# Where eight attention units divide by their softmax sums: on the exponentials, or on the outputs

## The chip, the cores and the metric

One Trainium2 chip, one core. The metric is device time in microseconds (us) of one execution, and the kernel before takes 1225.23 us (median of three runs, 1224.18 to 1225.33). Engine names are those of the profile: PE is the matrix engine (PEld its weight loads), DVE the vector engine, ACT the scalar engine, POOL the GpSimd engine, SP the queue that issues most DMAs.

## The reference, cut to what matters

The kernel computes a two-layer encoder trunk over 1024 positions of width 1024. Layer 0 mixes with differential attention (A, 4 heads of width 128) and sliding-window attention (B, 8 heads). Layer 1 mixes with chunked attention over a band of nine chunks of 64 positions (C, 16 heads of width 64). The change touches C alone:

```python
def chunked_relpos_attention(q, k, v, rel_table):      # per chunk c of 64 queries
    s = jnp.einsum('bqhd,bkhd->bhqk', qb, kb).astype(jnp.float32) * scale + bias
    valid = (c * CHUNK - pad + j) >= 0
    s = jnp.where(valid, s, NEG)
    p = jax.nn.softmax(s, axis=-1)
    return jnp.einsum('bhqk,bkhd->bqhd', p.astype(vb.dtype), vb)
# around it, layer 1:
    proj = jnp.einsum('bsd,de->bse', h, w_in_c[i])
    qc, kc, vc, gc = jnp.split(proj, 4, axis=-1)
    y = jnp.einsum('bse,ed->bsd', yc * jax.nn.silu(gc), w_out_c[i])
    x = x + rms_norm(y, post_norm_g[l])
```

The softmax is exp(s - max) divided by its row sum, and the division may stand before or after the product with v.

## The kernel before, in words

**Units.** The work is cut into 20 units: A0 to A3, B0 to B7 and C0 to C7. A C unit is one pair of heads over all 1024 positions. It has 16 items, one for each head h and each tile t of 128 queries, in the order (h0,t0) (h0,t1) (h1,t0) (h1,t1) (h0,t2) and so on (`order`, L85). An item of a C unit sees one to five tiles of 128 keys, most of them five.

**Steps.** All engines walk through one list of steps, each engine in its own fixed order, and wait for one another by semaphores. A C unit starts every 20 steps. Items run in its steps 0 to 15, and steps 16 to 19 hold the projections of keys and queries for the next unit. The pipeline of an item that is scored in step s, for a unit that is not "deferred":

- PE scores it in step s (`score`, L1309, matmuls at L1339) from q and k into PSUM.
- DVE adds the bias and finds the row minimum of the negated scores in its step s+1 (`lowest`, L1757, instruction L1771, into e_sb). ACT takes the exponential in its step s+1 (`exp`, L1443, L1447) and sums the rows into `total`.
- DVE in its step s+2 takes the reciprocal of the sum (L1783) and multiplies the exponentials by it in place (`normalise`, L1775, L1787).
- PE transposes the tiles in step s+3 (`turn`, L1273, L1306) into PSUM `turned`. ACT copies them rounded (L1480) and DVE keeps the remainder (L1836), both in step s+4.
- For each head and pair of query tiles PE multiplies by v one step after the second transpose (`times_v`, L1231, L1259). ACT and DVE then add the two halves of the result into `o_sb` (L1495, L1844).

For a "deferred" unit (`deferred`, L55) the multiplication at L1787 does not happen. The transposes come one step earlier, in step s+2, and the product with v with them. For each pair of query tiles, that is four times in a C unit, once both heads are there:

- DVE takes four reciprocals in one instruction (`denominators`, L1798, L1811).
- ACT spreads them over 256 columns (`widen`, L1514, L1520, into `rec_wide`).
- PE transposes these in two instructions (`turn_rec`, L1263, L1270) into the half of `pv_ps` that the product with v is not about to use.
- DVE multiplies `o_sb` by them (`times_rec`, L1813, L1819).

B0 to B7, C0 and C7 are deferred before. C1 to C6 are not.

**The order within a step on PE** is written out at L1366 to L1389: its share of the projections (`project`, L1126), one product with the output weights of the unit before (`spare_use`, L1140, matmuls L1137), the transposes of one item, the scores of one item, `turn_rec`, the product with v, and in the last step of a unit the transposes of the next unit's v (L1294).

**Between two C units.** In step 20 DVE keeps the remainder of v (L1831). In step 21 it multiplies the finished `o_sb` by the gate (`gated`, L1869, L1886), then ACT rounds it (`hi_of_gated`, L1497, L1512) and DVE takes the remainder (`gated_lo`, L1889, L1897). The first product with the output weights of the finished unit stands in step 4 of the next unit, and it waits for two things: that remainder, and the unit's output weights. Those weights are loaded by SP (L860) into a buffer that comes free with the last output product of the step before (step 19), and POOL splits them into a rounded part and a remainder (`split`, L967, one instruction at L971 and four at L978):

```python
            if x.what == "out":
                for u, w in zip(x.units, x.blocks):
                    if new(w_ready, PRO_SPLITS + w.n + 1):
                        pe.wait_ge(w_ready, PRO_SPLITS + w.n + 1)
                    if new(s_ylo, gate_of(u, x.row) + 1):
                        pe.wait_ge(s_ylo, gate_of(u, x.row) + 1)
```

On ACT the gated rounding of step 21 stands behind the first exponential of the unit and ahead of the second. On DVE the gated product stands behind item 0's row minimum and ahead of item 1's.

Of the kernel before, what the change touches and what calls it, by code (L numbers as in the profile page):

```python
# [33 lines left out]
            C=dict(q=0, k=1024, v=2048, g=3072))  # L34
# [5 lines left out]
class Unit:  # L40
# [12 lines left out]

    @property
    def deferred(self):  # L55
        return self.kind == "B" or self.kind == "C" and self.i in (0, 7)

    def slope(self, h):
        if self.kind == "A":
# [37 lines left out]
B = [Unit("B", i, 80 + 8 * i) for i in range(8)]  # L97
BRIDGE = 11
C = [Unit("C", i, 80 + 64 + BRIDGE + 20 * i) for i in range(8)]
# [1965 lines left out]
```

## Time and profile before

| | before |
|---|---|
| median of 3 runs | 1225.23 us |
| the profiled execution, its own time | 1223.95 us |
| its span, first to last instruction | 1222.2 us |
| PE busy | 1182.2 us (97%) |
| DVE busy | 804.6 us (66%) |
| ACT busy | 588.9 us (48%) |
| POOL busy | 432.8 us (35%) |
| granted PE clock, mean | 0.995 |

The span is what the instructions fill, and the execution's own time is 1.75 us more. The four engines run side by side, so their busy times are not to be added. Matmuls overlap in the records: a 128x512 matmul is shown with some 0.39 us, but the next one starts 0.23 us after it, so what a matmul costs PE is read from the distance between two starts. The C units lie from about 592 us to the end, and C1 to C6 start at about 669, 749, 827, 906, 984 and 1063 us, C7 at 1141.5 us.

### The profile page before, as it was taken

Reading aid. Unit: us, or ns where it says so; the run is one execution under the profiler, and the core shown is the slowest. Engines: PE = TensorE matmul, PEld = TensorE weight load, DVE = VectorE, ACT = ScalarE, POOL = GpSimd, SP = SyncE. Lnnn points to the kernel's source line nnn. Section 1 sums busy time; section 2 is a strip of 40 time slices with the busy share of each in tenths; the row PEclk is TensorE's granted clock in tenths of the full one; section 3 lists DMA queues with packets and bytes.
Section 4 is the critical chain, followed back from the end, with each engine's and each line's share of the span. In section 5 each row is a group of like instructions: output and inputs, shape, how many; then the busy total and the mean of one; then the engine's idle time right before and its main releaser. Section 6 shows DMA issues by size and latency. Waiting matters only on the chain.

```text
span 1222.2 us, 17651 instructions
## 1 busy us (share of the span) xinstructions
PE 1182.2 (97%) x6492; PEld 1006.7 (82%) x6492; DVE 804.6 (66%) x1708; ACT 588.9 (48%) x1296; POOL 432.8 (35%) x557
## 2 busy tenths in 40 slices
PE   7999999999999999898999999999999999999995
PEld 6988888888888887787788888888888888888873
DVE  5464765757767768867553866848658577585585
ACT  5554444434444556655454444534434444454463
POOL 5333214133172465556752114124141241412312
PEclk9999999999999999999999999999999999999998
DMA  6261101011021153245221102011020110201026
GB/s 197 67 192 44 60 18 52 18 53 35 18 87 53 51 156 104 69 127 155 61 77 58 34 21 71 18 56 53 18 74 19 56 53 19 73 18 57 18 47 109
DMA packets 93559, 78.42 MB, mean 64 GB/s; under 512 B 3073, under 2 KB 83969, under 8 KB 93474
## 3 DMA queue, kind: packets, MB, share of 16 engines
q1 hardware_dynamic: 92466, 73.63, 19.9%
q0 software_dynamic: 1008, 3.67, 1.9%
q8 instruction: 52, 0.85, 0.3%
q14 instruction: 33, 0.27, 0.1%
HBM read 68.85 MB, written 13.68 MB: 68 GB/s over the span
## 4 chain that ended last, share of the span: by engine, by line
PE 48%; DVE 2%; issue 1%; ACT 1%; POOL 1%; POOLq 0%; DVEq 0%; ACTq 0%
PE dense L1126 25%; PE dense L1137 7%; PE pv_ps L1259 6%; PE scores L1339 4%; PE turned L1306 4%; PE turned L1294 0%; DVE pT_lo L1836 0%; ACT k_hh L1440 0%; DVE e_sb L1771 0%; POOL w_lo L978 0%; POOL rowstat L1004 0%; DVE fin L2032 0%; PE scores L1137 0%; ACT junk L1622 0%; POOL rowstat L1001 0%
## 5 line engine op out<-in xcount | busy, mean ns | idle before, releaser
L1126 PE MATMUL dense<-hT_hi,w_hi 128*128 128x512 f32 x880 | 350.5, 398 | 0.0
L1126 PE MATMUL dense<-hT_lo,w_hi 128*128 128x512 f32 x880 | 344.6, 392 | 0.0
L1126 PE MATMUL dense<-hT_hi,w_lo 128*128 128x512 f32 x880 | 344.2, 391 | 0.0
L971 POOL TENSOR_SCALAR w_hi<-w_f 128x1024 fp32r<-128x1024 f32 x86 | 93.0, 1081 | 642.4 <-PE dense L1126 585.2
L978 POOL TENSOR_TENSOR w_lo<-w_f,w_hi 128x256 fp32r<-128x256 f32 x344 | 264.8, 801 | 7.2
L1447 ACT ACTIVATE e_sb<-e_sb,low 128x256 f32<-128x256 f32 (+7 forms) x256 | 170.3, 665 | 172.5 <-DVE low L1771 170.1
L1480 ACT ACTIVATE pT_hi<-turned 128x640 fp32r<-128x640 f32 (+3 forms) x224 | 117.2, 523 | 165.3 <-PE pv_ps L1259 94.5
L1126 PEld LDWEIGHTS dense<-hT_hi,w_lo 128*128 128x128 f32 x880 | 165.4, 188 | 36.6
L1126 PEld LDWEIGHTS dense<-hT_hi,w_hi 128*128 128x128 f32 x880 | 166.0, 189 | 26.1 <-issue 0.3
L1126 PEld LDWEIGHTS dense<-hT_lo,w_hi 128*128 128x128 f32 x880 | 166.2, 189 | 25.1
L1836 DVE TENSOR_TENSOR pT_lo<-turned,pT_hi 128x640 fp32r<-128x640 f32 (+3 forms) x224 | 133.5, 596 | 39.1 <-ACT pT_hi L1480 38.9
L1771 DVE CUSTOM_DVE_ANT_0 e_sb<-scores,bias 128x640 f32<-128x640 f32 (+3 forms) x192 | 131.4, 685 | 41.8 <-PE scores L1339 39.9
L1259 PE MATMUL pv_ps<-pT_hi,v_st 128*128 128x256 f32 x536 | 128.5, 288 | 1.7 <-DVE pT_lo L1836 1.7
L1339 PE MATMUL scores<-k_hh,q_st 128*128 128x384 f32 (+3 forms) x352 | 126.0, 358 | 0.7 <-DVE low L1771 0.6
L1306 PE MATMUL turned<-ident,e_sb 128*128 128x128 f32 x744 | 118.1, 273 | 1.7 <-DVE pT_lo L1836 1.3
L1306 PEld LDWEIGHTS turned<-ident,e_sb 128*128 128x128 f32 x744 | 92.7, 140 | 29.8 <-DVE pT_lo L1836 5.5
L1259 PE MATMUL pv_ps<-pT_lo,v_st 128*128 128x256 f32 x456 | 117.1, 283 | 0.0
L1339 PE MATMUL scores<-k_l,q_st 128*128 128x384 f32 (+3 forms) x352 | 107.7, 315 | 0.0
L1259 PEld LDWEIGHTS pv_ps<-pT_hi,v_st 128*128 128x128 f32 x536 | 97.6, 191 | 3.9 <-DVE pT_lo L1836 2.5
L1697 DVE TENSOR_TENSOR k_l<-dense,k_hh 64x512 fp32r<-64x512 f32 x48 | 33.0, 688 | 94.2 <-ACT k_hh L1440 93.7
L1691 DVE SCALAR_TENSOR_TENSOR q_st<-dense,q_st 64x512 fp32r<-64x512 f32 x60 | 41.4, 689 | 79.6 <-ACT q_st L1434 79.2
L1735 DVE TENSOR_TENSOR y<-dense,y 128x512 f32<-128x512 f32 x108 | 74.2, 687 | 23.9 <-PE dense L1137 23.0
(215 smaller groups left out, 1796.7 us busy)
## 6 DMA issues: line engine op xcount, KB each, us to landing
w_f<-in_w_in_c SPq DMA_DIRECT2D x37, 512.0 KB, 4.1
w_f<-in_w_in_ab SPq DMA_DIRECT2D x34, 512.0 KB, 3.9
rel_tiles_dram<-rel_rows_dram SPq DMA_DIRECT2D x1, 5120.0 KB, 23.8
bias<-rel_tiles_dram SPq DMA_DIRECT2D x8, 640.0 KB, 5.5
y<-in_x SPq DMA_DIRECT2D x8, 512.0 KB, 8.0
hT_lo_f<-in_x SPq DMA_DIRECT2D x8, 512.0 KB, 7.2
out_x<-y SPq DMA_DIRECT2D x8, 512.0 KB, 3.9
w_f<-in_w_out_c SPq DMA_DIRECT2D x8, 512.0 KB, 3.7
```

Source lines behind the costliest of these rows:

```text
L971: ts(hi, src, 1.0, 1.0, ALU.mult, ALU.mult).then_inc(w_hi_done, 1)
L978: last = tt(lo[:, h, cols], src[:, h, cols], hi[:, h, cols], ALU.subtract)
L1126: last = mm(dense[:, x.n % 2, :], lhs[:, d * P:(d + 1) * P], rhs[:, d, x.f * HALF:(x.f + 1) * HALF], start=i == 0, stop=i == 23)
L1137: last = mm(bank, lhs[:, c:c + P], rhs, start=not begun and m == n == 0, stop=m == len(parts) - 1 and n == 2)
L1259: last = mm(pv_ps[:, p.n % 2, :], v_st[:, which, kt, :], p_part[:, kt - p.t + 6 - pT_set(p), :], start=i == 0 and m == 0, stop=i == p.coun ...
L1306: last = nc.tensor.transpose(turned[:, at0:at0 + P], e_sb[:, e0:e0 + P], ident[:])
L1339: last = mm(scores[:, at0:at0 + w], q_st[:, it.h, c:c + P], k_part[:, kh, key:key + w], start=i == 0, stop=i == 1)
L1447: copy(e, e, ACT.Exp, scale=-1.0, bias=stat_col(low, it.j), accum_out=stat_col(total, it.j)).then_inc(s_exp, 1)
L1480: copy(pT_parts(pv)[0][:, r, q], turned_tile(x), ACT.Copy).then_inc(s_thi, 1)
L1735: last = tt(into, dense[:, 2, :], into, ALU.add)
L1771: nc.vector.tensor_tensor_reduce(out=e_of(it), in0=scores[:, it.off:it.off + it.n * P], in1=bias_of(it), scale=-u.slope(it.h), scalar=star ...
L1836: tt(lo[:, r, q], turned_tile(x), hi[:, r, q], ALU.subtract).then_inc(s_tlo, 1)
```

## The change

The property that decides which units are deferred now names every C unit. Everything else follows from it when the step lists are built (L234, L244, L255).

```diff
     @property
     def deferred(self):
-        return self.kind == "B" or self.kind == "C" and self.i in (0, 7)
+        return self.kind == "B" or self.kind == "C"
```

So in C1 to C6 the instructions at L1783 and L1787 go, those at L1811, L1520, L1270 and L1819 come, and transposes and products with v stand one step earlier.

## Rows read from the trace of the kernel before

**Rows 1.** Stretch of C5: its length, busy PE, PEld, DVE, ACT, POOL, then clock.

```profile
984.00:1062.00 78.00, 78.00 (x426) 66.68 (x425) 53.02 (x117) 35.66 (x74) 21.59 (x27) 1.00 0.14 43
```

**Rows 2.** Who PE waited for, from 590 to 1135 us (the one row).

```profile
PE dense L1137 <- DVE y L1733: 0.4, 1, 0.4
```

**Rows 3.** DVE groups of C5, 984 to 1062 us: count, busy us, mean ns.

```profile
L1787 DVE TENSOR_SCALAR e_sb<-e_sb,rec 128x640 f32<-128x640 f32 (+4 forms) x16 | 8.8, 552 | 0.6
L1783 DVE RECIPROCAL rec<-total 128x1 f32<-128x1 f32 x16 | 2.4, 153 | 0.0
```

**Rows 4.** Groups of the whole trace, shapes kept apart.

```profile
L1270 PE MATMUL pv_ps<-ident,rec_wide 128*128 128x128 f32 x48 | 9.2, 272 | 0.0
L1819 DVE TENSOR_TENSOR o_sb<-o_sb,pv_ps 128x256 f32<-128x256 f32 x24 | 10.1, 421 | 2.8 <-DVE o_sb L1844 0.5
L1811 DVE RECIPROCAL rec<-total 128x4 f32<-128x4 f32 x8 | 1.3, 168 | 0.0
L1520 ACT ACTIVATE rec_wide<-rec 128x256 f32<-128x256 f32 x24 | 9.9, 412 | 4.2 <-DVE rec L1811 3.7
```

**Rows 5.** Timeline of PE in C0: start us, length us, instruction.

```profile
627.73 0.38 PE L1270 MATMUL pv_ps<-ident,rec_wide 128*128 128x128 f32 x2
627.86 0.36 PE L1259 MATMUL pv_ps<-pT_hi,v_st 128*128 128x256 f32 x1
```

**Rows 6.** Timeline of PE from C3's last step into C4.

```profile
903.60 0.28 PE L1259 MATMUL pv_ps<-pT_hi,v_st 128*128 128x256 f32 x1
...
905.03 1.04 PE L1294 MATMUL turned<-ident,vT 128*128 128x128 f32 x8
...
912.10 0.27 PE L1306 MATMUL turned<-ident,e_sb 128*128 128x128 f32 x1
...
913.58 0.39 PE L1126 MATMUL dense<-hT_hi,w_lo 128*128 128x512 f32 x1
913.89 0.47 PE L1137 MATMUL dense<-w_hi,yT_hi 128*128 128x512 f32 x1
```

**Rows 7.** Timeline of SP and POOL over the same stretch.

```profile
903.79 0.34 SPq L860 DMA_DIRECT2D w_f<-in_w_out_c  x1
...
904.31 2.82 POOL L978 TENSOR_TENSOR w_lo<-w_f,w_hi 128x256 fp32r<-128x256 f32 x4
907.81 1.06 POOL L971 TENSOR_SCALAR w_hi<-w_f 128x1024 fp32r<-128x1024 f32 x1 [0.68 <-DMA w_f<-in_w_out_c]
908.95 4.84 POOL L978 TENSOR_TENSOR w_lo<-w_f,w_hi 128x256 fp32r<-128x256 f32 x4
```

**Rows 8.** Timeline of DVE and ACT over the same stretch.

```profile
905.77 0.69 DVE L1735 TENSOR_TENSOR y<-dense,y 128x512 f32<-128x512 f32 x1
907.16 1.23 DVE L1831 TENSOR_TENSOR v_st<-turned,v_st 128x1024 fp32r<-128x1024 f32 x1 [0.70 <-ACT v_st L1463]
909.08 1.69 DVE L1886 SCALAR_TENSOR_TENSOR o_sb<-o_sb,gate 128x1024 f32<-128x1024 f32 x1
911.90 1.30 DVE L1897 TENSOR_TENSOR yT_lo<-o_sb,yT_hi 128x1024 fp32r<-128x1024 f32 x1 [0.39 <-ACT yT_hi L1512]
...
910.80 1.06 ACT L1512 ACTIVATE yT_hi<-o_sb 128x1024 fp32r<-128x1024 f32 x1 [1.11 <-DVE o_sb L1886]
911.77 0.49 ACT L1447 ACTIVATE e_sb<-e_sb,low 128x256 f32<-128x256 f32 x1
```

**Rows 9.** The same POOL group two boundaries later (C5 to C6).

```profile
1066.01 4.84 POOL L978 TENSOR_TENSOR w_lo<-w_f,w_hi 128x256 fp32r<-128x256 f32 x4
```

**Rows 10.** Timeline of PE, from C0 into C1 and from C6 into C7.

```profile
673.88 0.39 PE L1126 MATMUL dense<-hT_hi,w_lo 128*128 128x512 f32 x1
674.18 0.33 PE L1339 MATMUL scores<-k_hh,q_st 128*128 128x128 f32 x1
...
1144.97 0.39 PE L1126 MATMUL dense<-hT_hi,w_hi 128*128 128x512 f32 x1
1145.46 0.44 PE L1339 MATMUL scores<-k_hh,q_st 128*128 128x384 f32 x1
```

## The prediction

> **What bounds the kernel now.** I read the stretches of the C units first. From 984 to 1062 us, about the length of C5, PE is busy for 78.00 of 78.00 us while DVE has 53.02 and ACT 35.66 [rows 1]. PE's granted clock is 1.00 there. The waits of PE say the same from the other side: over all of C0 to C6 they hold one row, 0.4 us [rows 2]. So in C1 to C6, where the change acts, PE is the bound and is fed without a gap. Work that leaves DVE returns at most what PE waits for, which is next to nothing. Whatever is added to PE, or makes it wait, lengthens the kernel by its full amount, because nothing behind it is idle to catch up. Then I read the timeline of PE, SP, POOL, DVE and ACT over one boundary between two units, C3 to C4 [rows 6 to 8], because this is where the order of the work is changed most.
>
> **What goes.** In each of six units DVE loses 16 multiplications (8.8 us) and 16 reciprocals (2.4 us) [rows 3], 11.2 us a unit and 67 us together. All of it lies beside PE's work, so I count nothing for it. A few small waits of PE go with it. The 0.4 us [rows 2] is a wait for DVE's addition into y in C1's step 5. PE also starts some 0.1 to 0.2 us late at the same place of three later units, and the transposes of C1's first item wait for a multiplied tile. I put all of these at -1.2 us, and the bounds are 0 and -1.5.
>
> **What comes, on DVE and ACT.** Four times a unit, 24 times in all, DVE gets a reciprocal of four columns (0.168 us) and a product of 128x256 (0.421 us), and ACT a spreading copy (0.412 us) [rows 4]. That is 14.1 us of DVE against 67 removed, and 9.9 us of ACT, which is idle for more than half of the stretch [rows 1]. I count both at nothing. They are hidden by PE's projections, and if that cover were gone the largest single piece would be the 0.42 us on the way to the next product with v (a rival below).
>
> **What comes, on PE: the turned reciprocals.** The records give 272 ns to each of the two transposes [rows 4], but records on PE overlap. What counts is by how much the next instruction starts later: the pair starts at 627.73 and the product with v behind it at 627.86 [rows 5], so a pair costs 0.13 us. 24 pairs are **3.1 us**, all on the path.
>
> The Trainium skill (TensorE: Matmul & The Clock Gate, Part 4: PE-mode transpose) gives a transpose of 128x128 about 275 ns in a kernel's context. The record's length agrees with it, the distance of the starts does not. By the page's figure as a price the term would be 13.2 us in place of 3.1, by the start distances it is 3.1. That reading is a rival below.
>
> **What moves: the last product with v of a unit.** Transposes and products come one step earlier. In the steady part of a unit each step keeps its content on PE: six projection matmuls, one output product, one item's transposes, one item's scores, and every second step a product with v. The short step between two transposes (the one without a product) had just enough time for row minimum, remainder and transposes, and it now has more, since the multiplication no longer stands ahead of them on DVE. Nothing is counted for these steps.
>
> At the end of a unit it is different. The last product with v stood in step 19, between the last output product and the transposes of the next v: 903.60 to 905.03, 1.43 us [rows 6]. Now it stands in step 18, so PE arrives at everything in the next unit 1.43 us earlier as seen from the end of the step-19 output product. Other engines do not come earlier with it. That output product frees the weight buffer. SP issues the load of the finished unit's output weights at 903.79, POOL starts at 907.81 behind the DMA, and its four remainders last from 908.95 to 913.79 [rows 7]. PE needs these weights for the first output product in step 4, which starts at 913.89, 0.31 us behind the matmul before it where 0.23 is usual [rows 6]: it is already on the edge. The start of this chain hangs on an instruction that the change leaves in place.
>
> POOL's group takes 4.84 us where the same group takes 2.82 with DVE otherwise occupied [rows 7]. In that stretch DVE has two products with two operands in SBUF, L1886 with 1.69 us and L1897 with 1.30 us [rows 8], and each holds one POOL instruction up by about 1 us. Both remain. The gated product starts earlier, in the middle of POOL's first instruction, and I expect both still to meet POOL. The group lasts 4.84 us in another boundary also [rows 9].
>
> So in the changed kernel PE resumes at the same 913.89, with 1.43 us less work done in between and one more pair of transposes (those of item 1, now in step 3, 0.13 us as in [rows 5]). The loss is 1.43 - 0.13 = 1.3 us at most for one boundary.
>
> The other chain to step 3 and 4 gives the lower bound. PE wants to transpose item 1 where it transposed item 0, 912.10 - 1.43 = 910.67 [rows 6]. It needs the exponential of item 1, which ACT runs behind the rounding of the gated output (910.80, then 911.77 [rows 8]), and that waits for the gated product on DVE. The remainder of v (907.16) can start only 0.7 us earlier, since an addition into y of 0.69 us from 905.77 stands ahead of it on DVE [rows 8], and the addition of the last product's halves, about 0.4 us, is gone from between. The gated product then starts near 909.08 - 0.7 - 0.4 = 908.0, ends near 909.4, 1.4 us earlier than before, and item 1's exponential is finished near 911.1. PE loses 0.4 us by this chain alone. The two are in series on PE, so the later one decides: between 0.4 and 1.3 us. I take 1.2, near the upper end, because the buffer, the DMA and POOL's own work do not move. What is late next is the weights' remainder, not the exponential. The boundaries C1 to C2, up to C5 to C6, are five: **6.0 us**.
>
> C0 to C1 and C6 to C7 are different. C0 was deferred before, so nothing of its end moves, but C1's first two items are transposed a step earlier. PE's scores already start at 674.18, 0.30 us behind the matmul before them [rows 10], held by item 0's minimum. The transposes behind them wait for exponentials that end some 0.5 us later, twice, so about +1.0 us. Into C7 the last product of C6 moves away. The scores of item 1 start at 1145.46, 0.49 us behind the matmul before [rows 10], and would wait for the minimum of item 0 a little longer, +0.3 us. C7 needs C6's weights only in its step 8.
>
> **Sum:** 3.1 + 6.0 + 1.3 - 1.2 = 9.2 us. The profiled execution has 1223.95 us, so it would be 1233.1. The median lies 1.28 above that execution, and the forecast for a median is 1234.4 us.
>
> **The rivals.** *Only the transposes.* If POOL's remainders do not meet the two DVE products any more, they end up to 2 us earlier and the boundary costs nothing but the exponential's 0.4 us or less. With the small gains this is 3.1 + 0 to 2.0 + 1.3 - 1.2, 3.2 to 5.2 us if the exponential counts, and down to 2 us if that is off as well, some 1227.2 to 1230.4 us. For it speaks that PE's other waits are so small. Against it, that the DMA and POOL are tied to step 19. Chance 0.15.
>
> *Faster.* The relief of DVE would have to reach PE at one place: the remainder of a transposed item (L1836), on which the next transposes wait. It decides if PE's records hide waits there. Were a tenth of the 67 us taken from DVE on this path, it would be -6.7 + 3.1 = -3.6, 1221.6 us. Against it: 78.00 of 78.00 busy [rows 1] and a single 0.4 us [rows 2]. Chance 0.03.
>
> *A new wait in each pair.* The product with v that follows a `turn_rec` waits for DVE's multiplication by the reciprocals. If its 0.421 us [rows 4] came on top 24 times, the time would be 10.1 us more, 1244.5. In C0 this wait exists and PE has no row for it [rows 2]. Chance 0.05.
>
> *Transposes at their full length.* 48 x 0.272 = 13.1 us in place of 3.1 [rows 4] gives 1244.4. The 0.13 us of [rows 5] speak against it. The page named above would have it so. Chance 0.02.
>
> **The numbers.** The forecast has 0.75. Its own range is 1231 to 1237 us, and down to 1228 takes in most of the first rival. I close the upper end at 1239, which leaves the last two out. A measurement of this kernel can tell about 0.2%, 2.5 us, from no change. Faster is the second rival, 0.03. Within 0.2% is the lower part of the first, 0.05. The rest, 0.92, is slower.
>
> **What would show it.** PE's busy matmuls at L1270 go from 48 to 96. DVE's busy time falls by some 50 us and the span grows all the same. At each of five boundaries PE shows an idle stretch before L1137 or L1306, of together more than 1 us, and in the first C step 4 of a unit the end of L978 lies just ahead of L1137. Within a unit, from step 5 on, PE has no wait. I am wrong if the five boundaries are free of waits (then it is near 1228), or if L1270 or the L1259 behind it shows waits in mid-unit.

## The result and the profile after

The changed kernel takes 1234.34 us (median of four runs, 1233.45 to 1235.39) against 1224.96 us of the kernel before in the same session. The ratio is 1.0079, its 95% interval 1.0063 to 1.0094. It is slower by 9.4 us, and the forecast was 1234.4. The profiled execution has 1233.45 us and a span of 1231.7 us. The sum came out right, but not because each of its terms did. Two of them, the price of a pair and the boundaries, were off in opposite directions. A third, the small waits that go, was larger than I allowed for. The runs below put sizes on them. Of the eight executions of the first run without reciprocals, three took 1475 to 4238 us and are left out of its median below.

First the busy times of the changed kernel, from its page, and the transposed reciprocals from its groups (engine, count, busy us, mean ns):

```profile
PE 1189.1 (97%) x6540; PEld 1013.1 (82%) x6540; DVE 763.0 (62%) x1564; ACT 594.1 (48%) x1320; POOL 430.6 (35%) x557
...
L1270 PE MATMUL pv_ps<-ident,rec_wide 128*128 128x128 f32 x96 | 18.3, 272 | 0.0
```

DVE gave up 41.6 us of its 804.6 and the kernel became longer. (The prediction had some 50, and by the sum of the records it is 52.8. Neighbouring records on DVE overlap, and the busy time counts that once.) PE has 48 matmuls more, all at L1270, where 48 became 96 as against [rows 4].

Who PE waited for from 590 to 1145 us, where [rows 2] has one row of 0.4 us:

```profile
PE dense L1137 <- issue: 2.0, 2, 1.0
PE turned L1306 <- ACT e_sb L1447: 1.6, 5, 0.5
PE dense L1294 <- DVE hT_lo L1747: 0.2, 1, 0.2
```

The two places named in the prediction are there: the transposes of the first items, which wait for ACT's exponential, and the first output product of a unit. "Issue" means that the view found no releaser. The boundary from C3 to C4 shows what it was. PE, then POOL, then DVE and ACT, to be laid beside [rows 6 to 8] (what follows the step-19 output product starts at 909.33 here and at 903.60 there, so everything is to be read 5.73 us later):

```profile
909.33 1.03 PE L1294 MATMUL turned<-ident,vT 128*128 128x128 f32 x8
...
918.14 0.39 PE L1126 MATMUL dense<-hT_hi,w_lo 128*128 128x512 f32 x1
919.55 0.47 PE L1137 MATMUL dense<-w_hi,yT_hi 128*128 128x512 f32 x1 [1.02 <-issue]
```

```profile
909.52 0.34 SPq L860 DMA_DIRECT2D w_f<-in_w_out_c  x1
...
913.57 2.00 POOL L971 TENSOR_SCALAR w_hi<-w_f 128x1024 fp32r<-128x1024 f32 x1 [0.70 <-DMA w_f<-in_w_out_c]
915.66 3.79 POOL L978 TENSOR_TENSOR w_lo<-w_f,w_hi 128x256 fp32r<-128x256 f32 x4
```

```profile
913.45 1.22 DVE L1886 SCALAR_TENSOR_TENSOR o_sb<-o_sb,gate 128x1024 f32<-128x1024 f32 x1
...
915.79 1.68 DVE L1897 TENSOR_TENSOR yT_lo<-o_sb,yT_hi 128x1024 fp32r<-128x1024 f32 x1 [0.78 <-ACT yT_hi L1512]
```

The v transposes now follow the output product directly, at 909.33. Before, a product with v of 1.43 us stood between. POOL's remainders end at 915.66 + 3.79 = 919.45 and PE's output product starts at 919.55, 1.18 us later than the 0.23 us rhythm would have it. The gated remainder on DVE had been done since 917.47. So PE waited for the weights, as forecast.

The boundary from C1 to C2 goes another way:

```profile
756.27 0.40 PE L1126 MATMUL dense<-hT_hi,w_lo 128*128 128x512 f32 x1
756.96 0.33 PE L1306 MATMUL turned<-ident,e_sb 128*128 128x128 f32 x1 [0.29 <-ACT e_sb L1447]
...
758.63 0.40 PE L1126 MATMUL dense<-hT_hi,w_lo 128*128 128x512 f32 x1
759.11 0.47 PE L1137 MATMUL dense<-w_hi,yT_hi 128*128 128x512 f32 x1
```

```profile
753.20 1.05 POOL L971 TENSOR_SCALAR w_hi<-w_f 128x1024 fp32r<-128x1024 f32 x1 [0.35 <-DMA w_f<-in_w_out_c]
754.34 4.67 POOL L978 TENSOR_TENSOR w_lo<-w_f,w_hi 128x256 fp32r<-128x256 f32 x4
...
753.42 1.90 DVE L1886 SCALAR_TENSOR_TENSOR o_sb<-o_sb,gate 128x1024 f32<-128x1024 f32 x1
```

Here POOL's first instruction came 0.22 us ahead of the gated product instead of 0.12 us behind it. It took 1.05 us and not 2.00, but it stretched the gated product to 1.90 us, and everything behind that product (rounding, item 1's exponential) is late. PE waits 0.46 us for the exponential and 0.25 us for the weights. (These sizes are start distances: 756.96 - 756.27 = 0.69 us, where 0.23 is usual. The view's 0.29 is only the part in which no matmul record runs.) The two waits are not independent. POOL's last remainder ends 9.71 us after the start of the v transposes (759.01 - 749.30), against 10.12 us from C3 to C4 (919.45 - 909.33), and PE goes on right behind it both times. So the weights decide the sum of the waits, 0.7 or 1.2 us, and the wait for the exponential lies inside it. By start distances the five boundaries cost 0.71, 0.69, 1.18, 0.73 and 1.19 us, **4.5 us** in all. In C1 the first two items wait 0.68 and 0.35 us for their exponentials. All the small waits that stood in C1 to C6 before are gone: 0.9 us in C1, 0.1 to 0.3 us in each of the others, **1.9 us** in all.

### The profile page after: what moved, and what is told of

The parts are those of the page before. It is cut to its first block, busy times and chain, and to the rows that moved or that the text cites. A ratio compares the mean times of both kernels' runs of the same rounds, so it can differ in the third digit from the quotient of the medians.

```text
span 1231.7 us, 17687 instructions
## 1 busy us (share of the span) xinstructions
PE 1189.1 (97%) x6540; PEld 1013.1 (82%) x6540; DVE 763.0 (62%) x1564; ACT 594.1 (48%) x1320; POOL 430.6 (35%) x557
## 4 chain that ended last, share of the span: by engine, by line
PE 47%; DVE 3%; issue 1%; ACT 1%; POOLq 0%; POOL 0%; DVEq 0%; ACTq 0%
PE dense L1126 24%; PE dense L1137 6%; PE pv_ps L1259 6%; PE turned L1306 4%; PE scores L1339 4%; DVE o_sb L1886 1%; PE pv_ps L1270 1%; DVE q_st L1691 0%; ACT yT_hi L1512 0%; DVE e_sb L1771 0%; DVE pT_lo L1836 0%; ACT q_st L1434 0%; DVE fin L2032 0%; PE scores L1137 0%; PE scores L1189 0%
## 5 line engine op out<-in xcount | busy, mean ns | idle before, releaser
L971 POOL TENSOR_SCALAR w_hi<-w_f 128x1024 fp32r<-128x1024 f32 x86 | 95.7, 1112 | 656.5 <-PE dense L1126 599.2
```

What stands on the lines that cost most here:

```text
L971: ts(hi, src, 1.0, 1.0, ALU.mult, ALU.mult).then_inc(w_hi_done, 1)
```

## The experiments

Every kernel was timed against the kernel before on the same chip. The changed kernel's own figures are those above.

**Both parts apart.** The change does two things to C1 to C6: it adds the pairs of turned reciprocals, and it moves transposes and products a step earlier. The first run keeps the pairs and puts the steps back:

```diff
-            g_ = Turned("p", u_, -1, it_.step + (2 if u_.deferred else 3), item=it_, ...
+            g_ = Turned("p", u_, -1, it_.step + (2 if u_.deferred and not (u_.kind == "C" and 0 < u_.i < 7) else 3), item=it_, ...
```

> The division stays on the outputs in all C units, but in C1 to C6 the transposes and the products with v stand in their old steps, so the last product with v of a unit is back in its step 19. Theory (my reading of the changed kernel's trace): the 24 pairs of turned reciprocals cost 0.22 us each, 5.2 us, because the second matmul behind a pair also starts 0.08 us late, and the boundaries between units cost some 4.5 us. Then this kernel is 5.2 - 0.8 = 4.4 us above the kernel before, about 1229.4 us, and PE waits for nothing at the five boundaries. As I predicted the terms (3.1 us for the pairs, 6.0 us for the boundaries): 3.1 - 0.8, about 1227.2 us. Rival, a new wait in each pair: no gain against the changed kernel, about 1234 us.

Measured: 1230.61 us, ratio 1.0045 (1.0032 to 1.0058), 5.5 us over the kernel before. The waits at the boundaries are gone, and others of the old kind are a little larger:

```profile
PE dense L1137 <- DVE y L1735: 0.9, 4, 0.3
PE dense L1137 <- DVE y L1733: 0.2, 1, 0.2
```

By start distances the waits in C1 to C6 are 3.1 us together, 0.3 to 0.5 us in step 5 of each unit, and they were 1.9 us in the kernel before. That is 1.2 us more, where my theory had 0.8 us less. Taken from the 5.5 us it leaves some 4.3 us for the 24 pairs, more than the 3.1 predicted. The interval of this run alone doesn't part the two. The rival with a wait in each pair is out.

The second run keeps the early steps and drops the pairs:

```diff
-                if u_.deferred and h_ == 1:
+                if u_.deferred and h_ == 1 and not (u_.kind == "C" and 0 < u_.i < 7):
                     RECS.append((len(RECS), it_, pv_))
...
-                          len(RECS) - 1 if u_.deferred else -1, u_.step(16) + 5, u_.step(16) + 6))
+                          len(RECS) - 1 if u_.kind == "C" and u_.i == 0 else -1, u_.step(16) + 5, u_.step(16) + 6))
```

> The changed kernel without the reciprocals in C1 to C6: no reciprocal, no spreading copy, no pair of transposes, no product with them, so the outputs of these units stay undivided. Transposes and products with v stand early. Theory: only the boundaries are left, 1234.3 - 5.2 = 1229.1 us. By the predicted price of a pair: 1234.3 - 3.1 = 1231.2 us. Rival, a new wait in each pair (0.42 us): 1224 to 1226 us.

> The same kernel as e2_norec once more, for an undisturbed profile: about 1229.1 us, PE waits at the five boundaries as in the changed kernel (4.5 us together) and nowhere else in C1 to C6.

Measured: 1228.82 us, ratio 1.0031 (1.0019 to 1.0043), and in the second session 1230.11 us, ratio 1.0041 (1.0027 to 1.0054). The rows are those of the second session, PE's waits and then one boundary (C3 to C4):

```profile
PE dense L1137 <- issue: 5.2, 5, 1.0
PE turned L1306 <- ACT e_sb L1447: 0.7, 2, 0.5
```

```profile
917.79 0.39 PE L1126 MATMUL dense<-hT_hi,w_lo 128*128 128x512 f32 x1
919.23 0.47 PE L1137 MATMUL dense<-w_hi,yT_hi 128*128 128x512 f32 x1 [1.04 <-issue]
...
913.12 2.13 POOL L971 TENSOR_SCALAR w_hi<-w_f 128x1024 fp32r<-128x1024 f32 x1 [0.59 <-DMA w_f<-in_w_out_c]
915.33 3.79 POOL L978 TENSOR_TENSOR w_lo<-w_f,w_hi 128x256 fp32r<-128x256 f32 x4
```

The early steps alone cost 3.7 to 5.0 us, with nothing added to PE. I expected 4.5 us of boundary waits. They are 1.19 to 1.20 us each here by start distances, 6.0 us. At all five POOL's first instruction is the one held up (it ends 6.2 us after the start of the v transposes each time) and the gated product takes 1.22 us. At four of them the gated product starts first. From C4 to C5 POOL's record starts 0.01 us ahead and POOL pays all the same, so the records don't settle the order when they are that close. Each boundary has the size that I had forecast.

The third run drops the pairs and puts the steps back too (both edits together):

> Both parts undone, without the old multiplication: C1 to C6 are divided nowhere, transposes and products stand in their old steps. Theory and prediction alike: DVE's multiplications were hidden, only the small waits of PE go, about 0.8 us less than the kernel before, 1224.1 us. Rival, the relief of DVE is worth time: 1221 us or less.

Measured: 1223.60 us, ratio 0.9988 (0.9979 to 0.9997). 67 us of multiplications and reciprocals taken from DVE are worth 1.5 us. Its distance to the first run, 1230.61 - 1223.60 = 7.0 us, is what the division on the outputs does without the moved steps: the pairs' own cost and the waits in step 5.

**The price of a pair.**

```diff
-            for o in range(2):
+            for o in (0, 1, 0, 1) if p.u.kind == "C" and 0 < p.u.i < 7 else (0, 1):
                 last = nc.tensor.transpose(pv_ps[:, 1 - p.n % 2, o * P:(o + 1) * P], rec_wide[:, o * P:(o + 1) * P], ident[:])
```

> The changed kernel with each pair of turned reciprocals in C1 to C6 made twice (four transposes with the same result). Theory: a transpose costs PE 0.109 us, a pair 0.22 us, so 24 x 0.22 = 5.2 us more, 1239.5 us. By the price that I predicted (0.13 us a pair) 3.1 us more, 1237.4 us. By the records' full length (0.27 us each) 13 us more, 1247.4 us.

Measured: 1239.14 us, ratio 1.0116 (1.0102 to 1.013), 4.8 us over the changed kernel's median. The intervals alone don't part 5.2 from 3.1 us. The units do. The v transposes that begin a boundary follow each other, in this kernel and in the changed one:

```profile
750.32 1.03 PE L1294 MATMUL turned<-ident,vT 128*128 128x128 f32 x8
...
831.18 1.03 PE L1294 MATMUL turned<-ident,vT 128*128 128x128 f32 x8
```

```profile
749.30 1.03 PE L1294 MATMUL turned<-ident,vT 128*128 128x128 f32 x8
...
829.34 1.03 PE L1294 MATMUL turned<-ident,vT 128*128 128x128 f32 x8
```

A unit takes 80.86 us against 80.04, 0.82 us for four pairs, with boundary waits of the same size (0.74 and 0.71 us by start distances). The same measure over all of C1 to C6, from the v transposes ahead of C1 to those ahead of C7, gives the price twice. The waits are start distances again:

| kernel | C1, us | C2 to C6, us | PE's waits in both | the rest |
|---|---|---|---|---|
| before | 79.50 | 392.60 | 1.9 | 470.2 |
| changed | 80.26 | 400.90 | 5.5 | 475.7 |
| pairs in the old steps | 79.97 | 397.80 | 3.1 | 474.7 |
| early steps, no pairs (second session) | 79.40 | 397.77 | 7.0 | 470.2 |
| old steps, no pairs | 79.14 | 391.63 | 0.6 | 470.2 |
| pairs twice | 81.13 | 404.98 | 5.4 | 480.7 |

Without waits, the three kernels that have no pairs in C1 to C6 agree at 470.2 us. The changed kernel has 5.5 us more, 0.23 us a pair, and the doubled pairs add 5.0 us, 0.21 us a pair. Why the 0.13 us of [rows 5] was too little is seen one instruction further on, in the changed kernel:

```profile
628.12 0.38 PE L1270 MATMUL pv_ps<-ident,rec_wide 128*128 128x128 f32 x2
628.26 0.36 PE L1259 MATMUL pv_ps<-pT_hi,v_st 128*128 128x256 f32 x1
628.46 0.28 PE L1259 MATMUL pv_ps<-pT_lo,v_st 128*128 128x256 f32 x1
628.58 0.28 PE L1259 MATMUL pv_ps<-pT_hi,v_st 128*128 128x256 f32 x1
```

The first matmul behind the pair starts early, 0.14 us after it, and the second only 0.20 us later, where 0.12 is usual. The pair delays the queue by 0.14 + 0.08 = 0.22 us. So [rows 5] was read rightly, and it was one instruction short.

**Moving what waits.** If the weights are what PE waits for, a later first output product must remove exactly that part:

```diff
-    out_steps((C[i_],), even_plan(C[i_ + 1].start + 4, 16, 16))
+    out_steps((C[i_],), even_plan(C[i_ + 1].start + 4, 16, 16) if not i_ else even_plan(C[i_ + 1].start + 5, 16, 15))
```

> The changed kernel with the output products of C1 to C5 starting in step 5 of the next unit instead of step 4 (16 products in 15 steps). Theory: this takes away the wait for the weights' remainder (0.25 us at three boundaries, 1.18 us at two) and leaves the wait for item 1's exponential (0.46 us at three). So 3.1 us less than the changed kernel, 1231.2 us, and PE has no wait at L1137 near the boundaries. Rival, it is the remainder of the gated output and not the weights that PE waits for, or a wait at another place takes over: 1233 to 1234 us.

Measured: 1231.19 us, ratio 1.0051 (1.0038 to 1.0064). The waits at L1137 are gone and those for the exponential are left (two in C1, and 0.5 to 0.7 us at three boundaries by start distances):

```profile
PE turned L1306 <- ACT e_sb L1447: 2.0, 5, 0.5
```

If the gated product is what delays the exponential, one could move it ahead of item 0's row minimum:

```diff
-        GATES.append(Gate(u_, len(GATES), u_.step(16) + 5, slice(0, SEQ), PVS[-1],
-                          len(RECS) - 1 if u_.deferred else -1, u_.step(16) + 5, u_.step(16) + 6))
+        e_ = 1 if u_.kind == "C" else 0
+        GATES.append(Gate(u_, len(GATES), u_.step(16) + 5 - e_, slice(0, SEQ), PVS[-1],
+                          len(RECS) - 1 if u_.deferred else -1, u_.step(16) + 5 - e_, u_.step(16) + 6 - e_))
```

> The changed kernel with the gated product, its rounding and its remainder one step earlier in C0 to C6, ahead of the first row minimum of the next unit. Theory: two chains make PE wait at a boundary. Item 1's exponential behind the gated rounding (0.46 us at three boundaries, 1.0 us in C1) goes away here. The weights' remainder on POOL stays, and with less in common with DVE it ends 0.5 us or more earlier. So 2 to 4 us less than the changed kernel, 1230.5 to 1232.3 us. Rival, the weights alone decide and POOL does not end earlier: PE waits as long at the first output product as it did at both places, 1234 us.

Measured: 1241.39 us, ratio 1.0132 (1.0119 to 1.0146), 7 us slower than the changed kernel. A miss, and neither theory had it. I had looked at item 1 only. PE's waits, then DVE at one boundary (this kernel's lines are one higher):

```profile
PE turned L1307 <- ACT e_sb L1448: 9.4, 11, 2.4
```

```profile
756.41 1.22 DVE L1887 SCALAR_TENSOR_TENSOR o_sb<-o_sb,gate 128x1024 f32<-128x1024 f32 x1
757.54 0.28 DVE L1772 CUSTOM_DVE_ANT_0 e_sb<-scores,bias 128x128 f32<-128x128 f32 x1
...
758.74 1.67 DVE L1898 TENSOR_TENSOR yT_lo<-o_sb,yT_hi 128x1024 fp32r<-128x1024 f32 x1 [0.91 <-ACT yT_hi L1513]
```

The gated product now stands ahead of item 0's minimum and the remainder ahead of item 1's. Both exponentials are late, and PE waits for both. The wait for the weights is gone, but by start distances PE waits 1.27 and 0.45 us at each of five boundaries and 2.55 us in C1, 11.2 us in all against 5.5 in the changed kernel. The rest of the 7 us is the clock: from 679 to 682 us, behind the long wait in C1, PE's granted clock is 0.50 (1.2 in place of 2.4 GHz), and 128x512 matmuls start 0.43 us apart instead of 0.23. By these distances that costs some 1.5 us, an estimate. In none of the other traces used here does the clock fall inside C1 to C6. That the wait brought it down is likely from this, but not tested.

The other direction, one step later for C0 to C5, together with the later output products:

```diff
-        GATES.append(Gate(u_, len(GATES), u_.step(16) + 5, slice(0, SEQ), PVS[-1],
-                          len(RECS) - 1 if u_.deferred else -1, u_.step(16) + 5, u_.step(16) + 6))
+        e_ = 1 if u_.kind == "C" and u_.i < 6 else 0
+        GATES.append(Gate(u_, len(GATES), u_.step(16) + 5 + e_, slice(0, SEQ), PVS[-1],
+                          len(RECS) - 1 if u_.deferred else -1, u_.step(16) + 5 + e_, u_.step(16) + 6 + e_))
...
-    out_steps((C[i_],), even_plan(C[i_ + 1].start + 4, 16, 16))
+    out_steps((C[i_],), even_plan(C[i_ + 1].start + 5, 16, 15))
```

> The changed kernel with the output products from step 5 on as in the run above (C0 too), and the gated product, its rounding and its remainder one step later in C0 to C5, behind item 1's row minimum and exponential. Theory: both chains are out of PE's way, and the boundaries cost 0.5 us or less in all. What stays over the kernel before are the pairs, 24 x 0.22 = 5.2 us, less the small waits gone: 1234.3 - 4.5 - 1 = about 1229 us. Rival, the remainder of the gated output, now a step later, is late in step 5: 1231 us or more.

Measured: 1232.83 us, ratio 1.0063 (1.005 to 1.0077). The theory's 1229 us is missed and the rival's number holds, though not by its mechanism:

```profile
PE pv_ps L1260 <- DVE pT_lo L1837: 1.5, 5, 0.5
PE turned L1307 <- ACT e_sb L1448: 0.5, 1, 0.5
```

The late remainder now holds up the transposed tiles' remainders on DVE, and PE's first product with v waits for them. C1's first wait, for item 0's exponential, is where it was.

**The other way round.** If pairs and the missing step-19 product are what costs, a kernel with fewer deferred units should win. C0 divides its exponentials too:

```diff
-        return self.kind == "B" or self.kind == "C"
+        return self.kind == "B" or self.kind == "C" and self.i == 7
```

> The other way round: C0 too divides its exponentials, only B0 to B7 and C7 are deferred. Theory: four pairs less, 0.9 us less than the kernel before, and C0's last product with v goes back to its step 19, which relaxes the boundary into C1 (0.3 to 0.8 us): 1223.5 us. Rival, the start of C0 behind the B units needs the earlier transposes: 1225 us or more.

Measured: 1222.93 us (11 runs) against 1225.43 (19 runs), ratio 0.9979 (0.997 to 0.9988). It is the fastest kernel here that still divides everywhere, 2.5 us below the kernel before (1.5 to 3.7 by the interval), where I expected 1.2 to 1.7. The one new wait, 0.3 us in C0, stays below what it saves:

```profile
PE dense L1126 <- DVE k_l L1697: 0.3, 1, 0.3
```

From C0's own v transposes to those ahead of C7 this trace is 1.3 us shorter than that of the kernel before (594.95 to 1140.73 there, 596.99 to 1141.44 here).

The same with the output products from step 5 on:

```diff
-    out_steps((C[i_],), even_plan(C[i_ + 1].start + 4, 16, 16))
+    out_steps((C[i_],), even_plan(C[i_ + 1].start + 5, 16, 15))
```

> The kernel of the run above with the output products of C0 to C5 from step 5 on. Theory: takes the small waits at the boundaries away too, 0.1 to 0.2 us each at three or four of them: 0.5 us less than the run above, 1223.0 us. Rival, two output products in step 5 make the DVE addition late: equal or slower than the run above.

Measured: 1228.57 us, ratio 1.0026 (1.0016 to 1.0035), 5.6 us worse than without it. PE's waits from 669 to 1145 us:

```profile
PE dense L1137 <- DVE y L1735: 3.7, 5, 0.7
PE dense L1137 <- DVE y L1733: 0.7, 1, 0.7
```

Two output products in one step need the same PSUM bank, and the addition between them is late, as the rival said. It is not DVE's load that makes it late. The wait of C2's step 5, DVE first, then PE:

```profile
758.95 0.29 DVE L1787 TENSOR_SCALAR e_sb<-e_sb,rec 128x128 f32<-128x128 f32 x1
759.72 0.69 DVE L1687 SCALAR_TENSOR_TENSOR gate<-gate,dense 128x512 f32<-128x512 f32 x1 [0.48 <-ACT gate L1419]
760.33 0.55 DVE L1771 CUSTOM_DVE_ANT_0 e_sb<-scores,bias 128x384 f32<-128x384 f32 x1
...
760.80 0.42 DVE L1836 TENSOR_TENSOR pT_lo<-turned,pT_hi 128x256 fp32r<-128x256 f32 x1
761.14 0.68 DVE L1735 TENSOR_TENSOR y<-dense,y 128x512 f32<-128x512 f32 x1
...
761.87 0.50 PE L1137 MATMUL dense<-w_hi,yT_hi 128*128 128x512 f32 x1 [0.73 <-DVE y L1735]
```

DVE stands idle for 0.48 us behind its last multiplication, until ACT has the gate, and no multiplication follows before the addition. In the changed kernel's schedule the same edit had no such wait: there the addition runs from 761.39 to about 762.07, and PE's second output product starts at 762.23. Counted from the start of ACT's gate (759.11 and 759.49), the addition ends after 2.7 us here and after 2.6 us there, but PE could go on after 1.9 us here and comes after 2.7 us there. In part that is the product with v, four matmuls and 0.49 us, which stands ahead of the two output products in the early steps and behind them in the old ones. The remaining 0.4 us I have not traced.

## Why the prediction was right, and where its terms were not

**PE is the bound.** Right. Without any division in C1 to C6, in the old steps, the kernel gains 1.5 us. The small waits were mis-sized, though: I had put them at 1.2 us with 1.5 as the bound. They were 1.9 us, and the changed kernel has none of them left.

**The pairs.** Right in kind, too small in size: 3.1 us predicted, 24 x 0.22 = 5.2 us by start distances and 5.5 us by the lengths of the units. The step that failed is "what counts is by how much the next instruction starts later". The next one starts early and the one behind it makes up for it.

**The boundaries.** Right in mechanism and place, too large in size: 6.0 us predicted, 4.5 us in the changed kernel. The upper chain (buffer, DMA, POOL) sets PE's start at all five. At two it costs 1.18 us as against 1.2 predicted. At three, POOL's first instruction comes ahead of the gated product and isn't held up by it. The weights come 0.4 us sooner and the exponential later, so PE waits for the exponential first, and the two waits are 0.7 us in sum. Without the pairs all five have the predicted size and cost 6.0 us. I had said that both DVE products would still meet POOL, and they do. That the order of two starts 0.1 to 0.2 us apart decides which side pays was not in the prediction.

**C0 to C1 and C6 to C7.** +1.0 us predicted for C1 and 1.03 measured. For C7's first scores I had +0.3, and nearly nothing came of it: they start 0.49 us behind the matmul before them in the kernel before [rows 10] and 0.52 us in the changed one. C7 as a whole is 0.2 us longer.

**The sum.** 5.5 + 4.5 + 1.0 + 0.2 - 1.9 = 9.3 us with the terms measured in the traces, 9.2 as predicted, 9.4 between the medians. I had put the pairs 2.4 us too low, the boundaries 1.5 us too high, and the small waits 0.7 us too low. These errors cancel nearly, so the agreement of the total to 0.2 us is luck. Each error alone would still have left the result within the range.

**The rivals.** "Only the transposes" is refuted by the two runs without pairs, which are 3.7 and 5.0 us slower than the kernel before. "Faster" is refuted by the 1.5 us above. "A new wait in each pair" is refuted by the run with the old steps, where the products with v have no such wait. "Full length" of the records, 0.27 us a transpose, would have made the doubled pairs cost 13 us, and they cost 4.8. The figure of about 275 ns in the Trainium skill (TensorE: Matmul & The Clock Gate, Part 4: PE-mode transpose) agrees with the length of a record, 272 ns, and not with the queue's delay, half a pair's 0.22 us.

Left open: why the kernel with C0 undeferred gains 2.5 us between medians where its trace explains 1.3, and how much a schedule made for deferred units could still give back, with row minima, gated product and remainder interleaved more finely than by whole steps.

## What to carry to other kernels

On an engine that is busy without a gap, relief elsewhere is worth only the small waits that it ends, and each added instruction costs its full price. Read that price from the starts of the next two instructions, not from its record and not from the next start alone. Check it against the length of a whole unit with and without them. When work moves from behind an event to ahead of it, ask which chains of other engines start at that event: they don't move along, and the moved work was their cover. A move that fixes the wait you look at can put another item behind the same instruction, so write down all queues at that place before choosing the step.

## What the runs showed of the hardware

POOL and DVE hold each other up, and the one that starts later pays. POOL's 128x1024 instruction (L971) takes 1.05 us, and 2.00 to 2.13 us when the gated product on DVE has just started. Where the gated product had 0.49 us to go (C2 to C3 without pairs), L971 took 1.41 us. The gated product takes 1.22 us, and 1.90 us when L971 started 0.22 us ahead of it. This agrees with the Trainium skill (GPSIMD Engine Reference, 1. Specifications), by which POOL's SBUF interfaces are shared with the vector engine, with contention against DVE instructions that have two inputs in SBUF. That the later starter bears the delay is from these rows.

The first matmul behind a pair of 128x128 transposes starts early, 0.14 us after the start of the pair, and the second is 0.08 us late. The delay of the queue is 0.11 us a transpose, whatever the record's 0.27 us say.

At a granted clock of 0.50 instead of 1.00, 128x512 matmuls start 0.43 us apart instead of 0.23.
